# Recurrence's block inverse on one Trainium2 core: the inverse's extension and its transpose's in separate banks

## What is computed

```python
def _rwkv7_scan(s0, r, w, k, v, a, b):
    def step(S, inp):
        r_t, w_t, k_t, v_t, a_t, b_t = inp
        sa = jnp.einsum('bhvk,bhk->bhv', S, a_t)
        S = S * w_t[:, :, None, :] + sa[..., None] * b_t[:, :, None, :] + v_t[..., None] * k_t[:, :, None, :]
        return S, jnp.einsum('bhvk,bhk->bhv', S, r_t)
    xs = tuple(jnp.moveaxis(t, 1, 0) for t in (r, w, k, v, a, b))
    s_fin, ys = lax.scan(step, s0, xs)
    return s_fin, jnp.moveaxis(ys, 0, 1)
```

## Time and profile before

| what | value |
|---|---|
| median of three runs | 3259.41 us (3255.51 to 3261.84) |
| the profiled execution's own time | 3247.96 us |
| its span | 3246.2 us |
| mean granted TensorE clock | 0.967 |
| busy share of the span | PE 94%, PE weight loads 72%, DVE 62%, ACT 46%, GpSimd 0% |
| DMA | 619.71 MB, mean 191 GB/s |
| first matmul of the first solve to last addition of the last inverse | 348 us to 685 us of the span |

### The profile page before, as it was taken

How to read it: one execution, slowest core, us unless ns; L and a number is a source line. 1 busy time by engine, 2 the same in 40 slices (tenths; PEclk the granted TensorE clock), 3 DMA queues, 4 the chain that set the end, 5 groups by cost and what they waited for, 6 DMA issues and landing times.

```text
span 3246.2 us, 70881 instructions
## 1 busy us (share of the span) xinstructions
PE 3035.9 (94%) x28960; PEld 2343.0 (72%) x28960; DVE 2022.0 (62%) x3676; ACT 1500.8 (46%) x2394; POOL 7.7 (0%) x17
## 2 busy tenths in 40 slices
PE   5988897989999989989999999999999999999998
PEld 3866684878989977643333333359988999998998
DVE  3768757565555552766666666666685666667566
ACT  3334223223444442646666666664447444445543
POOL 0000000000000000000000000000000000000000
PEclk8998898999999999989999999999999999999999
DMA  5232205004545552059999999955542555543454
GB/s 212 97 130 111 106 3 227 4 25 139 181 155 175 182 180 91 21 224 379 379 378 389 377 380 407 373 229 184 181 143 99 181 182 172 182 155 122 145 181 155
DMA packets 132792, 619.71 MB, mean 191 GB/s; under 512 B 14496, under 2 KB 18080, under 8 KB 98400
## 3 DMA queue, kind: packets, MB, share of 16 engines
q1 hardware_dynamic: 132048, 610.18, 51.5%
q0 software_dynamic: 528, 6.43, 0.5%
HBM read 615.50 MB, written 1.05 MB: 190 GB/s over the span
## 4 chain that ended last, share of the span: by engine, by line
PE 82%; DVE 10%; ACT 3%; DMA 2%; issue 1%; SPq 1%; DVEq 0%; ACTq 0%
PE ps L2443 21%; PE ps L310 16%; PE ps L311 16%; PE ps L312 16%; DMA ada_late<-wada 1%; PE ps L1777 1%; PE ps L864 1%; DVE w_lo L273 1%; PE ps L1774 1%; PE ps L1768 1%; PE ps L2454 1%; DVE tt L1865 1%; ACT w_hi L269 1%; DVE mxv L2157 1%; PE ps L792 0%
## 5 line engine op out<-in xcount | busy, mean ns | idle before, releaser
L273 DVE TENSOR_TENSOR w_lo<-w_raw,w_hi 128x1024 fp32r<-128x1024 f32 x529 | 646.3, 1224 | 598.3 <-ACT w_hi L269 594.7
L310 PE MATMUL ps<-a_hi,w_hi 128*128 128x256 f32 (+1 forms) x3012 | 899.1, 299 | 48.4 <-DVE a_lo L811 11.9
L311 PE MATMUL ps<-a_lo,w_hi 128*128 128x256 f32 (+1 forms) x3012 | 895.2, 297 | 0.0
L312 PE MATMUL ps<-a_hi,w_lo 128*128 128x256 f32 (+1 forms) x3012 | 894.4, 297 | 0.0
L269 ACT ACTIVATE w_hi<-w_raw 128x1024 fp32r<-128x1024 f32 x529 | 557.7, 1056 | 610.4 <-PE ps L312 556.3
L310 PEld LDWEIGHTS ps<-a_hi,w_hi 128*128 128x128 f32 x3012 | 578.2, 192 | 71.9 <-issue 45.4
L312 PEld LDWEIGHTS ps<-a_hi,w_lo 128*128 128x128 f32 x3012 | 573.0, 190 | 16.1
L311 PEld LDWEIGHTS ps<-a_lo,w_hi 128*128 128x128 f32 x3012 | 573.2, 190 | 15.2 <-issue 0.5
L2625 DVE COPY wx<-wset 128x512 f32 x1188 | 425.1, 422 | 223.1 <-PE ps L2443 208.0
L2565 ACT ACTIVATE wx<-wset 128x512 f32 x792 | 444.4, 621 | 214.7 <-PE ps L2443 206.3
L2443 PE MATMUL ps<-wx,xT 128*32 128x512 f32 x2640 | 377.6, 596 | 4.8 <-DVE wx L2625 4.8
(11 more groups left out here) (518 smaller groups left out, 3444.1 us busy)
## 6 DMA issues: line engine op xcount, KB each, us to landing
w_raw<-wstream SPq DMA_DIRECT2D x529, 512.0 KB, 3.3
wset<-wexp SPq DMA_DIRECT2D x264, 1024.0 KB, 7.8
ada_late<-wada SPq DMA_DIRECT2D x80, 512.0 KB, 6.2
ada_raw<-wada SPq DMA_DIRECT2D x16, 512.0 KB, 9.2
bia<-bias POOLq DMA_DIRECT2D x1, 4096.0 KB, 13.4
con<-consts SPq DMA_DIRECT2D x1, 1824.0 KB, 16.0
conb<-constsb POOLq DMA_DIRECT2D x1, 1224.0 KB, 5.7
hT<-ctxT SPq DMA_DIRECT2D x1, 1024.0 KB, 12.3
```

What stands on the lines that cost most here:

```text
L273: nc.vector.tensor_tensor(wlo[:, slot, :], raw[:, slot, :], whi[:, slot, :].bitcast(F32), ALU.subtract).then_inc(lo_ready.sem, 1)
L310: nc.tensor.matmul(out, lhs[0], rhs[0], start=start, stop=False, skip_group_check=skip)
L311: nc.tensor.matmul(out, lhs[0], rhs[1], start=False, stop=False, skip_group_check=skip)
L312: return nc.tensor.matmul(out, lhs[1], rhs[0], start=False, stop=stop, skip_group_check=skip)
```

## The change

The extension of T keeps its place in bank 2 + d and gets the signal `t_ps` for itself. The transpose's extension goes to bank 6 + d, with a signal of its own, `t1_ps`. DVE adds them in two instructions of 256 columns, each of which signals PE by its own completion: `lv_in` after T's, `t1_in` (or `tT_done` in the last level) after the transpose's. PE waits for `t1_in` only in front of the extensions of the next level. PE's order and the order of the directions stay. The two new signals take over two semaphores of earlier stages.

```diff
           "x_out": ("st_ps", 6), "slot_ps": ("g_ps", 8), "slot_sb": ("mb_rt", 1), "moe_free": ("mb_r", 1), "x_scaled": ("e1", 16),
+          "t1_ps": ("bc_ps", 16), "t1_in": ("wm", 16),
           "r_ready": ("e2", 16), "r_ps": ("dd", 16)}
@@ pe_solve
                 for d in range(2):
                     pe.wait_ge(*S("x_sb").next("pe"))
+                    if lv > 0:
+                        pe.wait_ge(*S("t1_in").next("pe"))
                     if lv < RLEV - 1:
                         heads_of(d, lambda d, m, e: nc.tensor.matmul(
                             ps[hp(e), 2 + d, col(m)], tt[hp(e), d, 1, m, :], xs[hp(e), d, m, :],
-                            start=True, stop=True))
+                            start=True, stop=True)).then_inc(*S("t_ps").one)
                     heads_of(d, lambda d, m, e: nc.tensor.matmul(
-                        ps[hp(e), 2 + d, col(m, 1)], xs[hp(e), d, m, :], tt[hp(e), d, 1, m, :],
-                        start=True, stop=True)).then_inc(*S("t_ps").one)
+                        ps[hp(e), 6 + d, col(m)], xs[hp(e), d, m, :], tt[hp(e), d, 1, m, :],
+                        start=True, stop=True)).then_inc(*S("t1_ps").one)
@@ dve_solve
                 for d in range(2):
-                    dve.wait_ge(*S("t_ps").next("dve"))
                     if lv < RLEV - 1:
-                        t2_ = tt[:, d, :, :, :].rearrange("p s m l -> p (s m) l")
-                        link(nc.vector.tensor_tensor(t2_, t2_, bank(2 + d, 0, 8), ALU.add))
-                        dve.sem_inc(S("lv_in").sem, 1)
-                    else:
-                        nc.vector.tensor_tensor(tt[:, d, 1, :, :], tt[:, d, 1, :, :], bank(2 + d, 1), ALU.add
-                                                ).then_inc(*S("tT_done").one)
+                        dve.wait_ge(*S("t_ps").next("dve"))
+                        nc.vector.tensor_tensor(tt[:, d, 0, :, :], tt[:, d, 0, :, :], bank(2 + d), ALU.add
+                                                ).then_inc(*S("lv_in").one)
+                    dve.wait_ge(*S("t1_ps").next("dve"))
+                    nc.vector.tensor_tensor(tt[:, d, 1, :, :], tt[:, d, 1, :, :], bank(6 + d), ALU.add
+                                            ).then_inc(*S("t1_in" if lv < RLEV - 1 else "tT_done").one)
```

## The result

| kernel | median, us | lowest to highest | ratio to the kernel before, 95% interval |
|---|---|---|---|
| before, 5 runs | 3259.86 | 3255.51 to 3263.51 | 1 |
| after, 5 runs | 3243.68 | 3234.18 to 3244.43 | 0.9942 [0.9925, 0.9959] |

The changed kernel is faster by 0.6%: 16 us between the medians, where 12.4 were forecast for the likeliest case, and 3243.7 us lies inside the range. By the means of the five runs each it is 19 us. The profiled execution took 3238.94 us, its span is 3237.1 us and its mean granted clock 0.966 (before: 3246.2 us and 0.967).

What follows compares the result with a forecast made beforehand. PE's waits in each level's 3.39 us loop through direction 1 were the bound; 3 x 0.33 + 0.575 = 1.56 us per solve, 12.5 for eight, less 0.1 for lower clock, gave 3259.4 − 12.4 = 3247.0 us, range 3239 to 3257.

Steps and rivals of the forecast that it cites:

- Where the time goes: Levels of the inverse: PE issues a group per 0.465 us; the 3.39 us loop through direction 1 becomes 3.06 through direction 0.
- The predicted signs: In the trace: T(0) every 3.0 to 3.1 us, X(0) and X(1) 0.46 apart, solve starts some 31.9 us apart.
- The sum: Per solve: three level periods save 0.33 us each and the last level 0.575, together 1.56 us; 12.4 us over all.
- the time from X(0)'s start to its copy: In a level's loop, from X(0)'s start on PE to ACT's copy: taken as 0.77 us, between 0.73 and 0.81.
- The second wait: PE's added wait for `t1_in` before the next level's extensions: between nothing and 0.06 us per level, taken as nothing.
- the bounds of 9.3 to 13.7: Total saving in us: 13.7 with 0.73 for X; 9.3 with 0.81 and 0.06 for PE's added wait.
- The clock: Heads of solves: falls to half clock in three of eight, about 5.2 us in all; could go either way by 3 us.
- The wait in front of X(1): Head of each solve: PE idles some 2.3 us while DVE prepares direction 1; the change leaves this alone.
- DVE's extra instruction: DVE's additions in a level: a pair takes 0.84 us instead of 0.69, hidden; uncovered, 9.9 us over 64 pairs.
- A: Levels: the copy's way hidden too, so 2.79 us a level, 19 us saved, 3240 us; chance 5%.
- B: Latent segment's preparation: DMAs set by time, or a group's signal much later than 0.81; 6.2 us saved, 3253; chance 10%.
- C: Moved solves fall into half clock in more levels, 5.1 us each; with ten such, 3267 us; chance 5%.

## Why the prediction was right

**Where the time goes.** Right. PE's issue of 0.465 us a group, X(0) behind four groups, and ACT's copy as the next thing late are all in the first fence. The predicted signs (T(0) every 3.0 to 3.1 us, X(0) and X(1) back to back, solves 31.9 us apart) came out at 3.03, back to back, and 31.78.

**The sum.** Right, and a little low. The mis-sized term was the time from X(0)'s start to its copy. 0.77 was taken as the middle of 0.73 and 0.81; it is 369.76 − 369.03 = 0.73, also with a group behind it. The second wait is free or nearly so: from the end of the copy (369.76 + 0.38 = 370.14) to T(0) it is 0.06, where 0.05 was taken. Three periods save 3 x 0.36 instead of 3 x 0.33, and a solve 1.69 us instead of 1.56: 13.5 us, inside the bounds of 9.3 to 13.7, and 13.2 at equal clock. The medians' 16 us are outside those bounds but inside the range with the clock; that they are higher than 13 is luck of the first runs, as is part of the agreement in the absolute number: 12.4 were taken off a median of 3259.4, while 59 later runs of the kernel before have a mean of 3254.9 and 11 of the changed kernel 3241.0.

**The clock.** Right that its falls at the heads of solves go either way, and close on the price of one, put at 1.5 to 2.2 us: it is 1.3 to 1.6 in solves 2 to 7 and 2.2 to 2.4 in the eighth. Low on how many: three of eight were taken from the one profile of the kernel before, and the changed kernel's two profiles have four and five. The wait in front of X(1), read as 2.3 us, is 2.4 in the first solve and 2.5 in the others.

**DVE's extra instruction.** DVE's busy time rose from 2022.0 to 2029.6 us, 7.6 against the 9.9 that 64 pairs cost by the durations (the addition 0.42 us, as taken). None of it shows on the path. The Trainium skill's advice in VectorE: DVE Perf Modes, section on the TRN2 errata, to tile Vector instructions at 512 elements or more, would have kept the slower kernel here. The price it names is real (0.84 us for two halves against 0.69 for the whole), but cutting the instruction brought the first half's result forward, and that brought 1.31 of the 1.69 us per solve.

**The rivals.** A, PE's issue floor, can't be reached by this change but was reached by another order (2.80 us). B, half of it swallowed by DMA, did not happen: the gain at equal clock is the levels' whole. C, levels at half clock, did not happen either: behind a fall at the head of a solve the granted clock is back at 1.00, as from 402 to 406 us. The Trainium skill (TensorE: Matmul & The Clock Gate, section A second HAM failure mode: psum-queue depth-cycling) reports of another kernel a clock that goes back and forth with short idle times and cycled banks; in these levels, with 0.15 us of idle time in front of T(0) and another bank at each group, the trace does not show it.

## What to carry to other kernels

On an in-order engine, write down the loop of each repeated step as a sum of issue times and waits, for each of the interleaved streams; the longest sum is the period, and an edit is worth only the distance to the next one. An early signal pays only if the waiting instruction is at the head of its queue when it comes: here cutting the addition in two gave three quarters of the gain and the separate signal one quarter, while moving X(0) forward past a group of the other direction brought the level down to PE's issue. Compare runs at equal clock when the effect is smaller than the clock's scatter.

## What was not expected of the hardware

Twenty-four idle matmuls per solve, 1.4 us of useless work, made the changed kernel 8.4 us faster. With one wait of 2.5 us at the head, the clock fell in 24 of 49 solves (the first seven of each profile); with work in that wait, in none of 49. The run's time follows the mean granted clock at 2.1 us for each 0.001, over kernels whose runs spread by 6 to 18 us.
